# Three quarters of an MLP: weight halves made one chunk earlier on ScalarE, two VectorE steps reordered, one pair of loads moved

## The chip, the cores and the metric

The kernel runs on one core of one Trainium2 chip. The metric is the device time of one execution in microseconds (us). A core has five engines with instruction queues of their own: TensorE (PE, matrix products), VectorE (DVE), ScalarE (ACT), GpSimd (POOL) and SyncE (SP, which here issues nearly all DMA transfers). Each works through its own queue in order; they meet only at semaphores.

## The reference

Two transformer-like blocks run one after the other on 512 tokens of width 1024, in float32. The change touches only the MLP of the first block:

```python
u = rms_norm(h, norm_mlp_g[l])
h = h + jnp.square(jax.nn.relu(u @ w_mlp1[l])) @ w_mlp2[l]   # 1024 -> 4096 -> 1024
```

Around it stand a convolution branch, a latent attention and a cross attention before, and in the second block a spatial gating, a dilated attention and three projections after. All results must hold to float32 accuracy.

## The kernel before, in words

**Products in three parts.** TensorE multiplies in a rounded 32-bit format (F32R). To keep accuracy each operand is split in a high half (rounded, written by ACT with a Copy into `wh`, `fh`, `sh`, `s4h`) and a low half (the rest, written by DVE with a subtraction into `wl`, `fl`, `sl`, `s4l`). Each product is then three matmuls: high by high, low by high, high by low.

**Weights in chunks.** Weights stream in chunks of 512 KB (128 x 1024 floats). SP loads a chunk into `raw` (two slots), ACT's `split(c)` makes the high half in `wh[:, c % 4]`, DVE's `lower(c)` the low half in `wl[:, c % 4]`, PE uses them. The waits between: a load waits until the chunk that was in its slot has been lowered; `split` waits for the landing and until PE has entered the chunk behind the slot's last user (`chunk_entered`); `lower` waits for `split`; PE waits for `lower` (`lo_made`).

**The MLP in quarters.** The 4096 inner columns are done in four quarters q = 0 to 3, each an up part (`up{q}`) and a down part (`down{q}`).

An up part has eight jobs m = 0 to 7. PE's job is 24 matmuls into bank `lin0` or `lin1` in turn. Then ACT takes the bank with a Relu into `ta` or `tb` (`to(...)`, which also frees the bank), DVE squares it into `tc` or `td`, ACT copies the high half into `fh`, DVE subtracts for `fl`. After each odd job DVE makes sums of the pair of activation tiles (`sums`, into `first_turned`), ACT copies their high halves (`fh`, `sh`, `s4h`), and DVE makes their low halves one job later (`sums_low`).

The down parts of quarters 0 to 2 (`seven`) use a Strassen-like scheme with seven products in place of eight, for which DVE also makes sums of pairs of weight tiles (`pair_sums(u, kk)`, kk = 0 to 3, three additions each). Such a down part has 14 chunks, called v0 to v13 here, of 12 matmuls each; v0, v2, v4, v6 are a raw tile, v1, v3, v5, v7 are a sum and half of a tile, v8 to v13 the rest. The raw tiles come over a ring of four slots (`raw2`, `raw3`, `raw[:, 1]`, `raw[:, 0]`; the trace calls them all `raw`), loaded by `seven_loaded(u, r)`, r = 0 to 11. v(2k) and v(2k+1) can be made only after pair_sums(k). PE's v1 writes both `lin` banks, so it also waits until both are free, which the Relu of jobs 6 and 7 does. The fourth quarter is plain.

**What sets the order.** All orders are written out by hand in the program of each engine. In the up part of quarters 0 to 2, chunk c+m is the one that job m uses, and c+8 is v0 of the down part. Before the change ACT's job m is: split(c+m+3), Relu, copy of `fh`, and after odd jobs the three copies of the sums. DVE's job m is: lower(c+m+3), in some jobs pair_sums, then sums_low, the square, sums, the low half. So v0, v1 and v2 are made within the up part, and v3 and on behind it.

Of the kernel before, what the change touches and what calls it, by code (L numbers as in the profile page):

```python
# [30 lines left out]
ACT = mybir.ActivationFunctionType  # L31
AX_X = mybir.AxisListType.X

P = 128
# [48 lines left out]
NORM_NO = {n: k for k, (n, _) in enumerate(NORMS)}  # L83
# [8 lines left out]
ADD0, _t = {}, 0  # L92
# [30 lines left out]
SEVENS = 3  # L123
# [26 lines left out]
def seven_lowered(u, r):  # L150

    return SEVEN0[u] + r + (r > 9) + 1


def seven_sum(u, kk, n):

    return SEVEN_SUMS * u + (3 * kk + n if n < 4 else 12 + kk + 1)
# [34 lines left out]
def build(nc, a, out):  # L192
    ctx = ExitStack()
    with ctx:
# [3 lines left out]
        def sb(name, shape, dt=F32, stack=ctx):  # L198
            return stack.enter_context(nc.sbuf_tensor(name, shape, dt))
# [14 lines left out]
        st = ExitStack()  # L214
# [105 lines left out]
        crows = sb("crows", [TAPS, CONV], stack=st)  # L320
        st.close()
        st = ExitStack()
        s4h = sb("s4h", [P, 4, 256], F32R, st)
        s4l = sb("s4l", [P, 4, 256], F32R, st)
        acc5 = sb("acc5", [P, 2, S], stack=st)
        raw2 = sb("raw2", [P, 1024], stack=st)
        st.close()
        st = ExitStack()
        xq = sb("xq", [P, XH, S], F32R, st)
# [191 lines left out]
        def _(sp):  # L521
# [98 lines left out]
            for q in range(4):  # L620
                c, _ = phase(f"up{q}")
                for m in range(DT):
                    if q and m < 2:
                        sp.wait_ge(sums_made, seven_sum(q - 1, 2 + m, 4))
                    load(c + m, a["w_mlp1"][0], q * FFQ + P * m, DT, P)
                    if 0 < q < SEVENS and m == 5:
                        for r in range(2):
                            sp.wait_ge(lo_made, seven_lowered(q - 1, 8 + r))
                            sp.wait_ge(sums_made, seven_sum(q - 1, r, 4))
                            seven_loaded(q, r)  # L630
                c, _ = phase(f"down{q}")
                rows = a["w_mlp2"][0][q * FFQ:(q + 1) * FFQ, :]
                if q == SEVENS:
                    for m in range(DT):
                        load(c + m, rows, P * m, DT, P)
                    continue
                for r in range(2 if q else 0, SEVEN_LOADS):
                    if r < 2:
                        sp.wait_ge(std_made, NORM_NO["mlp"] + 1)
                    elif r < 4:  # L640
                        sp.wait_ge(lo_made, c.static + r - 3)
                    else:
                        sp.wait_ge(lo_made, seven_lowered(q, r - 4))
                        if r % 2 == 0:
                            sp.wait_ge(sums_made, seven_sum(q, (r - 4) // 2, 3))
                    seven_loaded(q, r)
# [716 lines left out]
        def _(act):  # L1363
# [55 lines left out]
            def to(j, dst, func, rows=slice(0, P), n=S, **kw):  # L1419

                act.activation(dst, read(j)[rows, 0:n], func, **kw).then_inc(lin_freed[j.slot(2)], 1)
# [266 lines left out]
            def up(q):  # L1688
                c, j = phase(f"up{q}")
                for m in range(DT):  # L1690
                    if q == SEVENS or m == 0:
                        split(c + (m + 2))
                    if q < SEVENS:
                        split(c + (m + 3))
                    to(j + m, (ta, tb)[m % 2][:], ACT.Relu)
                    n = 256 if q < SEVENS and m % 2 == 0 else S
                    act.wait_ge(f_sq, DT * q + m + 1)
                    act.activation(fh[:, m, 0:n], (tc, td)[m % 2][:, 0:n], ACT.Copy).then_inc(f_high, 1)
                    if q < SEVENS and m % 2:
                        kk = m // 2  # L1700
                        act.wait_ge(s_made, 4 * q + kk + 1)
                        act.activation(fh[:, m - 1, 256:512], SF[:, 0, :], ACT.Copy)
                        act.activation(sh[:, kk, :, :], SF[:, 1:3, :], ACT.Copy)
                        act.activation(s4h[:, kk, :], SF[:, 3, :], ACT.Copy).then_inc(s_high, 1)
                    if q == 0 and m == 3:
                        norm_std("mlp")

            for q in range(4):
                up(q)
                c, _ = phase(f"down{q}")  # L1710
                if q < SEVENS:
                    for v in range(3, 10):
                        split(c + v)
                    if q == 0:
                        part_copied(0, SUM_X1, PART_X)
                        part_copied(1, SUM_Q1, PART_Q)
                    split(c + 10)
                    if q == 0:
                        part_copied(2, SUM_P, PART_P)
                        part_copied(3, SUM_R1, PART_R)  # L1720
                    for v in range(11, 16):
                        split(c + v)
                    if q == 0:
                        part_copied(4, SUM_X2, PART_X)
                        part_copied(5, SUM_Q2, PART_Q)
                        part_copied(6, SUM_R2, PART_R)
                    continue
                for m in range(DT):
                    if m == 0:
                        split(c + 2)  # L1730
                    if m < DT - 1:
                        split(c + (m + 3))
                    act.wait_ge(h_added, DT + m + 1)
                    wait(act, hsq_added, 2 * m + 1)
                    src = h[:, m, :]
                    gain_high(uh[:, m, :], src, both[:, m:m + 1])
                    act.activation(ta[:], src, ACT.Square).then_inc(hsq_made, 1)
                    act.activation(tb[:], src, ACT.Square, scale=col("final_norm_g", m)).then_inc(hsq_made, 1)
# [182 lines left out]
        def _(dve):  # L1921
# [493 lines left out]
            def up(q):  # L2415
                c, j = phase(f"up{q}")
                for m in range(DT):
                    if q == SEVENS or m == 0:
                        lower(c + (m + 2))
                    if q == 0 and m == 5:  # L2420
                        pair_sums(q, 0)
                    if q < SEVENS:
                        lower(c + (m + 3))
                    if 0 < q < SEVENS and m == 3:
                        pair_sums(q, 0)
                    if q < SEVENS and m == (5 if q else 6):
                        pair_sums(q, 1)
                    base = SEVEN_PARTS * SEVENS
                    if q == SEVENS and m == 0:
                        dve.wait_ge(part_taken, base)  # L2430
# [22 lines left out]
                    r_, whole, n = (ta, tb)[m % 2][:], (tc, td)[m % 2], 256 if q < SEVENS and m % 2 == 0 else S  # L2453
                    dve.tensor_tensor(whole[:], r_, r_, ALU.mult).then_inc(f_sq, 1)
                    dve.wait_ge(f_sq, DT * q + m + 1)
                    if q < SEVENS and m % 2:
                        sums(q, m // 2)
                    low(fl[:, m, 0:n], whole[:, 0:n], fh[:, m, 0:n], f_high, DT * q + m + 1, f_low)
# [17 lines left out]
            def seven(u):  # L2476

                c, _ = phase(f"down{u}")
                lower(c + 3)
                sums_low(u, 3)  # L2480
                pair_sums(u, 2)
                lower(c + 4)
                lower(c + 5)
                pair_sums(u, 3)
                for v in range(6, 10):
# [352 lines left out]
```

## Time and profile before

| | us |
|---|---|
| median of 3 runs (1355.49 to 1355.65) | 1355.64 |
| the profiled execution | 1355.72 |
| its span, first to last instruction | 1354.0 |
| PE busy in the span | 1327.3 (98%) |
| DVE busy | 1039.1 (77%) |
| ACT busy | 626.8 (46%) |
| mean granted TensorE clock | 0.996 |

The profile tells for each engine when it was busy and, from semaphore events, which instruction ended its idle time. A matmul's recorded duration (0.39 us) is longer than the distance between two starts (0.23 us), since matmuls overlap; distances of starts are what counts for time. Busy shares over the whole span say little of a single place: one has to look at the stretch in which PE stands still and read what ended each wait.

### The profile page before, as it was taken

What the parts mean: (1) busy time and instruction counts of PE and PEld (TensorE: products, weight loads), DVE (VectorE), ACT (ScalarE), POOL (GpSimd) and SP (SyncE); (2) the same over time, 40 slices, a digit from 0 to 9 for tenths busy, and PEclk for the clock granted to TensorE, in tenths of its full rate; (3) what the DMA queues carried; (4) which work ended last, traced back from release to release, by engine and by line L of the source; (5) the groups of instructions that cost most, each with busy time, mean ns of one, the idle gap of its engine ahead of it and who ended that gap; (6) DMA issues with size and microseconds to landing.
All of it is one profiled execution on the core that took longest, in us unless ns stands there. A gap on an engine that the chain in (4) does not pass through costs nothing.

```text
span 1354.0 us, 17136 instructions
## 1 busy us (share of the span) xinstructions
PE 1327.3 (98%) x6357; PEld 1085.4 (80%) x6357; DVE 1039.1 (77%) x1715; ACT 626.8 (46%) x1076; POOL 62.7 (5%) x60
## 2 busy tenths in 40 slices
PE   7999999999999899999999999999999999999998
PEld 6787877788888778788788888878888888888886
DVE  7868888885677766877887564598889988995685
ACT  7535655564555454434434544734333434333234
POOL 1000000102002000000001500000000000000000
PEclk9999999999999999999999999999999999999999
DMA  5333332243323234342333333322233223223332
GB/s 163 94 93 78 77 74 84 64 139 109 94 94 107 88 117 125 96 138 70 101 109 94 94 109 93 93 84 82 82 98 90 86 68 96 85 76 109 96 108 93
DMA packets 204340, 130.33 MB, mean 96 GB/s; under 512 B 21426, under 2 KB 190467, under 8 KB 204258
## 3 DMA queue, kind: packets, MB, share of 16 engines
q1 hardware_dynamic: 202642, 126.62, 32.1%
q10 hardware_dynamic: 1616, 2.62, 0.6%
q8 instruction: 51, 0.84, 0.3%
q14 instruction: 31, 0.25, 0.1%
HBM read 127.12 MB, written 2.10 MB: 95 GB/s over the span
## 4 chain that ended last, share of the span: by engine, by line
PE 86%; DVE 8%; ACT 4%; issue 2%; ACTq 0%; DVEq 0%
PE lin L757 21%; PE lin L761 20%; PE lin L760 20%; PE ob L1254 1%; PE sc L849 1%; PE sc L1113 1%; PE sc L1117 1%; PE sc L1116 1%; DVE wl L1965 1%; PE sc L1210 1%; PE sc L1213 1%; PE sc L1214 1%; ACT wh L1390 1%; PE tr L862 1%; PE ob L886 1%
## 5 line engine op out<-in xcount | busy, mean ns | idle before, releaser
L1965 DVE TENSOR_TENSOR wl<-raw,wh 128x1024 fp32r<-128x1024 f32 (+2 forms) x211 | 251.8, 1195 | 70.4 <-ACT wh L1413 69.4
L1413 ACT ACTIVATE wh<-raw 128x1024 fp32r<-128x1024 f32 (+2 forms) x211 | 214.8, 1020 | 92.9 <-DMA raw<-in_w_mlp_dram 23.3
L757 PE MATMUL lin<-uh,wh 128*128 128x512 f32 x624 | 250.4, 401 | 1.0 <-DVE ul L2037 0.9
L761 PE MATMUL lin<-uh,wl 128*128 128x512 f32 x624 | 243.4, 390 | 0.0
L760 PE MATMUL lin<-ul,wh 128*128 128x512 f32 x624 | 243.1, 390 | 0.0
L757 PE MATMUL lin<-vh,wh 128*128 128x512 f32 x512 | 202.6, 396 | 0.2 <-DVE te L2700 0.2
L760 PE MATMUL lin<-vl,wh 128*128 128x512 f32 x512 | 199.6, 390 | 0.0
L761 PE MATMUL lin<-vh,wl 128*128 128x512 f32 x512 | 199.3, 389 | 0.0
L757 PEld LDWEIGHTS lin<-uh,wh 128*128 128x128 f32 x624 | 117.2, 188 | 28.2 <-issue 3.8
L760 PEld LDWEIGHTS lin<-ul,wh 128*128 128x128 f32 x624 | 117.3, 188 | 24.9 <-issue 2.2
L761 PEld LDWEIGHTS lin<-uh,wl 128*128 128x128 f32 x624 | 117.1, 188 | 24.9
L757 PEld LDWEIGHTS lin<-vh,wh 128*128 128x128 f32 x512 | 96.2, 188 | 24.5 <-issue 4.2
L761 PEld LDWEIGHTS lin<-vh,wl 128*128 128x128 f32 x512 | 96.1, 188 | 20.3
L760 PEld LDWEIGHTS lin<-vl,wh 128*128 128x128 f32 x512 | 96.2, 188 | 18.9
L2658 DVE STREAM_TRANSPOSE first_turned<-logit 32x320 f32<-32x320 f32 x128 | 64.3, 503 | 2.2
L2658 DVE STREAM_TRANSPOSE second_turned<-logit 32x320 f32<-32x320 f32 x128 | 64.3, 502 | 1.8
L1460 ACT ACTIVATE logit<-logit,small 128x128 f32<-128x128 f32 (+1 forms) x96 | 53.3, 558 | 19.7 <-DVE small L2046 19.4
L2144 DVE SCALAR_TENSOR_TENSOR conv<-conv,taps 128x512 f32<-128x512 f32 x60 | 44.9, 748 | 0.0
L2144 DVE SCALAR_TENSOR_TENSOR te<-conv,taps,te 128x512 f32<-128x512 f32 x56 | 41.8, 747 | 0.0
L1390 ACT ACTIVATE wh<-raw 128x1024 fp32r<-128x1024 f32 x24 | 25.4, 1058 | 31.6 <-DVE raw L1932 22.1
L1950 DVE TENSOR_TENSOR wl<-raw,wh 128x1024 fp32r<-128x1024 f32 x24 | 29.4, 1224 | 7.7 <-ACT wh L1390 7.6
L2046 DVE CUSTOM_DVE_ANT_0 logit<-sc,bias 128x128 f32<-128x128 f32 (+1 forms) x64 | 28.7, 488 | 4.5 <-PE sc L849 4.0
(666 smaller groups left out, 2499.0 us busy)
## 6 DMA issues: line engine op xcount, KB each, us to landing
raw<-in_w_in_dram SPq DMA_DIRECT2D x100, 512.0 KB, 3.8
raw<-in_w_mlp_dram SPq DMA_DIRECT2D x64, 512.0 KB, 4.0
raw<-in_w_out_dram SPq DMA_DIRECT2D x16, 512.0 KB, 3.5
raw<-in_w_xkv_dram SPq DMA_DIRECT2D x8, 512.0 KB, 3.6
raw<-in_w_proj_b_dram SPq DMA_DIRECT2D x8, 512.0 KB, 3.7
raw<-in_w_proj_a_dram SPq DMA_DIRECT2D x8, 512.0 KB, 3.6
raw<-in_w_mlp_dram SPq DMA_DIRECT2D x12, 256.0 KB, 2.6
xtok<-in_x_dram ACTq DMA_DIRECT2D x4, 512.0 KB, 4.9
```

The source lines that it names most:

```text
L757: ins = pe.matmul(o, wh[:, slot, at], xh_, start=start, stop=False)
L760: pe.matmul(o, wh[:, slot, at], xl_, start=False, stop=False)
L761: return pe.matmul(o, wl[:, slot, at], xh_, start=False, stop=stop)
L849: ins = pe.matmul(sc[b][:, o:o + KEYS[q]], qt[:, q * P:(q + 1) * P], keys[:, 0:KEYS[q]], start=True, stop=True)
L1390: act.activation(high, raw_, ACT.Copy).then_inc(hi_made, 1)
L1413: act.activation(wh[:, c.slot(4), 0:size], raw[:, c.slot(2), 0:size], ACT.Copy).then_inc(hi_made, 1)
L1460: act.activation(p, p, ACT.Exp, bias=nmax[:, q:q + 1], scale=-1.0, accum_out=den[:, q:q + 1])\
L1950: dve.tensor_tensor(low_, raw_, high, ALU.subtract).then_inc(lo_made, 1)
L1965: dve.tensor_tensor(wl[:, c.slot(4), 0:size], raw[:, c.slot(2), 0:size], wh[:, c.slot(4), 0:size].bitcast(F32), ALU.subtract).then_inc(lo_ ...
L2046: dve.tensor_tensor_reduce(logit[:, LOFF[q]:LOFF[q] + KEYS[q]], banks[q][:, o:o + KEYS[q]], bias[:, S - KEYS[q]:S], 1.0, 3e38, ALU.add, AL ...
L2144: return dve.scalar_tensor_tensor(at, zt, tap_, at, ALU.mult, ALU.add)
L2658: ins = dve.transpose(BLOCKS[p][32 * k:32 * k + 32, :, 32 * q:32 * q + 32], probs[32 * q:32 * q + 32, :, k, :])
```

## The change

In the up parts of quarters 0 to 2:

- ACT makes the high half of the next chunk right behind each Relu instead of ahead of it, and that of chunk c+m+4 instead of c+m+3. v3 is made at job 7, and v4 behind the last copy of `fh`; the copies of the last activation sums stand behind v4.
- DVE's order in jobs 0 to 6 keeps lower(c+m+3) first. pair_sums(0) is at job 3 and pair_sums(1) at job 5 in all three quarters (in quarter 0 they were at jobs 5 and 6), and both stand behind that job's lower. In job 7 lower of v3 and pair_sums(2) now stand between the square and the activation sums.
- SP issues the first pair of raw tiles of quarter 0 at job 5's load, as in the other quarters, once the sum of squares of the norm is complete, instead of behind all eight loads and after the standard deviation. For this the buffer `raw2` was moved to another place of the shared memory region.

PE's, POOL's and the fourth quarter's programs are as before, and every engine has the same instructions in number and kind.

```diff
@@ the shared memory region
+        raw2 = sb("raw2", [P, 1024], stack=st)
         s4h = sb("s4h", [P, 4, 256], F32R, st)
         s4l = sb("s4l", [P, 4, 256], F32R, st)
         acc5 = sb("acc5", [P, 2, S], stack=st)
-        raw2 = sb("raw2", [P, 1024], stack=st)
@@ SP
                     load(c + m, a["w_mlp1"][0], q * FFQ + P * m, DT, P)
-                    if 0 < q < SEVENS and m == 5:
+                    if q < SEVENS and m == 5:
                         for r in range(2):
-                            sp.wait_ge(lo_made, seven_lowered(q - 1, 8 + r))
-                            sp.wait_ge(sums_made, seven_sum(q - 1, r, 4))
+                            if q:
+                                sp.wait_ge(lo_made, seven_lowered(q - 1, 8 + r))
+                                sp.wait_ge(sums_made, seven_sum(q - 1, r, 4))
+                            elif r == 0:
+                                sp.wait_ge(sq_added, ADD0["mlp"] + NTILES["mlp"] - 1)
                             seven_loaded(q, r)
...
-                for r in range(2 if q else 0, SEVEN_LOADS):
-                    if r < 2:
-                        sp.wait_ge(std_made, NORM_NO["mlp"] + 1)
-                    elif r < 4:
+                for r in range(2, SEVEN_LOADS):
+                    if r < 4:
                         sp.wait_ge(lo_made, c.static + r - 3)
@@ ACT
                     if q == SEVENS or m == 0:
                         split(c + (m + 2))
+                    if q < SEVENS and m == 0:
+                        split(c + 3)
+                    to(j + m, (ta, tb)[m % 2][:], ACT.Relu)
                     if q < SEVENS:
-                        split(c + (m + 3))
-                    to(j + m, (ta, tb)[m % 2][:], ACT.Relu)
+                        split(c + (m + 4))
                     n = 256 if q < SEVENS and m % 2 == 0 else S
                     act.wait_ge(f_sq, DT * q + m + 1)
                     act.activation(fh[:, m, 0:n], (tc, td)[m % 2][:, 0:n], ACT.Copy).then_inc(f_high, 1)
+                    if q < SEVENS and m == 7:
+                        split(c + 12)
...
-                    for v in range(3, 10):
+                    for v in range(5, 10):
                         split(c + v)
@@ DVE
-                    if q == 0 and m == 5:
-                        pair_sums(q, 0)
                     if q < SEVENS:
                         lower(c + (m + 3))
-                    if 0 < q < SEVENS and m == 3:
-                        pair_sums(q, 0)
-                    if q < SEVENS and m == (5 if q else 6):
-                        pair_sums(q, 1)
+                    if q < SEVENS and m in (3, 5):
+                        pair_sums(q, m // 4)
...
                     dve.wait_ge(f_sq, DT * q + m + 1)
+                    if q < SEVENS and m == 7:
+                        lower(c + 11)
+                        pair_sums(q, 2)
                     if q < SEVENS and m % 2:
                         sums(q, m // 2)
...
                 c, _ = phase(f"down{u}")
-                lower(c + 3)
+                lower(c + 4)
                 sums_low(u, 3)
-                pair_sums(u, 2)
-                lower(c + 4)
                 lower(c + 5)
                 pair_sums(u, 3)
```

ACT's rows at the end of quarter 1's up part, before: from the Relu of job 6 (`ta<-lin0`) on. `wh<-raw` is v2, `logit` and `raw` are v3, `raw2` is v4.

```order
L1421 ACTIVATE ta<-lin0 128x512
L1698 ACTIVATE fh<-tc 128x256
L1390 ACTIVATE wh<-raw 128x1024
L1421 ACTIVATE tb<-lin1 128x512
L1698 ACTIVATE fh<-td 128x512
L1702 ACTIVATE fh<-first_turned 128x256
L1703 ACTIVATE sh<-first_turned 128x512
L1704 ACTIVATE s4h<-first_turned 128x256
L1382 ACTIVATE wh<-logit 128x512
L1383 ACTIVATE wh<-raw 128x512
L1390 ACTIVATE wh<-raw2 128x1024
```

The same place on ACT now.

```order
L1422 ACTIVATE ta<-lin0 128x512
L1391 ACTIVATE wh<-raw 128x1024
L1701 ACTIVATE fh<-tc 128x256
L1422 ACTIVATE tb<-lin1 128x512
L1383 ACTIVATE wh<-logit 128x512
L1384 ACTIVATE wh<-raw 128x512
L1701 ACTIVATE fh<-td 128x512
L1391 ACTIVATE wh<-raw2 128x1024
L1707 ACTIVATE fh<-first_turned 128x256
L1708 ACTIVATE sh<-first_turned 128x512
L1709 ACTIVATE s4h<-first_turned 128x256
```

v2 stands behind the Relu of job 6 and no longer between that Relu's `fh` copy and the Relu of job 7; v3 and v4 stand ahead of the copies of the last sums.

DVE's rows at the same place, before: from the square of job 7 (`td<-tb`) to the low half of v4 (`wl<-raw2`). `first_turned` are the activation sums, `trig<-raw2,raw3` is the last addition of pair_sums(2).

```order
L2454 TENSOR_TENSOR td<-tb 128x512
L2402 TENSOR_TENSOR first_turned<-tc,td 128x256
L2403 TENSOR_TENSOR first_turned<-first_turned,tc 128x256
...
L1978 TENSOR_TENSOR fl<-td,fh 128x512
L1946 TENSOR_TENSOR wl<-logit,wh 128x512
L1947 TENSOR_TENSOR wl<-raw,wh 128x512
...
L2397 TENSOR_TENSOR s4l<-first_turned,s4h 128x256
L1930 TENSOR_TENSOR raw3<-raw2,raw3 128x512
L1932 TENSOR_TENSOR raw2<-raw2 128x512
L1934 TENSOR_TENSOR trig<-raw2,raw3 128x512
L1950 TENSOR_TENSOR wl<-raw2,wh 128x1024
```

The same place on DVE now.

```order
L2455 TENSOR_TENSOR td<-tb 128x512
L1951 TENSOR_TENSOR wl<-logit,wh 128x512
L1952 TENSOR_TENSOR wl<-raw,wh 128x512
L1935 TENSOR_TENSOR raw3<-raw2,raw3 128x512
L1937 TENSOR_TENSOR raw2<-raw2 128x512
L1939 TENSOR_TENSOR trig<-raw2,raw3 128x512
L2407 TENSOR_TENSOR first_turned<-tc,td 128x256
...
L1983 TENSOR_TENSOR fl<-td,fh 128x512
L1955 TENSOR_TENSOR wl<-raw2,wh 128x1024
L2400 TENSOR_TENSOR fl<-first_turned,fh 128x256
```

The low half of v3 and pair_sums(2) stand ahead of the activation sums, and the low half of v4 right behind the low half of the last activation tile.

## Rows read from the trace of the kernel before

**Rows 1.** The page: engines busy, and the chain that ended last.

```profile
PE 1327.3 (98%) x6357; PEld 1085.4 (80%) x6357; DVE 1039.1 (77%) x1715; ACT 626.8 (46%) x1076; POOL 62.7 (5%) x60
...
PE 86%; DVE 8%; ACT 4%; issue 2%; ACTq 0%; DVEq 0%
```

**Rows 2.** Stretches: the three seven-product down parts; length, then each engine's busy time, PEclk.

```profile
463.40:509.07 45.67, 40.22 (x170) 32.43 (x168) 32.40 (x47) 23.78 (x38) 0.00 (x0) 0.96 0.34 105
552.59:596.39 43.80, 40.75 (x170) 32.48 (x168) 35.75 (x53) 17.68 (x25) 0.00 (x0) 0.96 0.35 108
639.91:682.05 42.14, 39.07 (x170) 31.30 (x168) 35.19 (x53) 17.54 (x25) 0.99 (x2) 1.00 0.34 109
```

**Rows 3.** Timeline of PE: start, duration, instruction, idle time before it and its releaser.

```profile
469.90 0.76 PE L1113 MATMUL lin<-wh,sh 128*128 128x512 f32 x1 [3.62 <-ACT tb L1421]
481.60 0.47 PE L1113 MATMUL sc<-wh,fh 128*128 128x512 f32 x1 [1.83 <-DVE wl L1950]
...
562.20 0.50 PE L1113 MATMUL lin<-wh,sh 128*128 128x512 f32 x1 [0.95 <-DVE wl L1947]
567.24 0.47 PE L1113 MATMUL sc<-wh,fh 128*128 128x512 f32 x1 [2.03 <-DVE wl L1950]
...
569.28 0.63 PE L1116 MATMUL sc<-wh,fl 128*128 128x512 f32 x1
...
585.41 0.39 PE L1113 MATMUL tr<-wh,fh 128*128 128x512 f32 x1
...
596.39 0.39 PE L757 MATMUL lin<-uh,wh 128*128 128x512 f32 x1
```

**Rows 4.** Timeline of ACT, jobs 6 and 7 of quarter 1.

```profile
550.21 0.58 ACT L1421 ACTIVATE ta<-lin 128x512 f32<-128x512 f32 x1
553.55 0.42 ACT L1698 ACTIVATE fh<-tc 128x256 fp32r<-128x256 f32 x1 [2.76 <-DVE tc L2454]
553.87 1.05 ACT L1390 ACTIVATE wh<-raw 128x1024 fp32r<-128x1024 f32 x1
554.82 0.58 ACT L1421 ACTIVATE tb<-lin 128x512 f32<-128x512 f32 x1
```

**Rows 5.** Timeline of DVE, jobs 6 and 7 of quarter 1 and its down part.

```profile
550.34 0.69 DVE L1946 TENSOR_TENSOR wl<-vtok,wh 128x512 fp32r<-128x512 f32 x1 [1.76 <-ACT wh L1383]
...
556.81 0.42 DVE L2402 TENSOR_TENSOR first_turned<-tc,td 128x256 f32<-128x256 f32 x1
...
560.85 0.69 DVE L1946 TENSOR_TENSOR wl<-logit,wh 128x512 fp32r<-128x512 f32 x1 [1.76 <-ACT wh L1383]
...
565.87 1.23 DVE L1950 TENSOR_TENSOR wl<-raw,wh 128x1024 fp32r<-128x1024 f32 x1 [0.40 <-ACT wh L1390]
```

**Rows 6.** One line of the kernel, L536 (chunk loads), then L617 (raw tiles).

```profile
DMA to landing us min/median/max: 3.3/3.8/5.5
...
DMA to landing us min/median/max: 2.5/3.3/5.3
```

**Rows 7.** Timeline of ACT, POOL and DVE near the start of quarter 0.

```profile
425.04 0.60 ACT L1421 ACTIVATE ta<-lin 128x512 f32<-128x512 f32 x1 [1.27 <-PE lin L761]
...
428.38 1.06 ACT L1413 ACTIVATE wh<-raw 128x1024 fp32r<-128x1024 f32 x1 [1.56 <-DMA raw<-in_w_mlp_dram]
430.48 0.60 ACT L1421 ACTIVATE tb<-lin 128x512 f32<-128x512 f32 x1 [1.04 <-PE lin L761]
...
421.65 1.42 POOL L708 TENSOR_TENSOR logit<-logit,qt 128x512 f32<-128x512 f32 x1 [1.14 <-ACT qt L1432]
...
422.56 2.73 DVE L1965 TENSOR_TENSOR wl<-raw,wh 128x1024 fp32r<-128x1024 f32 x2 [0.66 <-ACT wh L1413]
...
446.82 3.35 DVE L2014 RECIPROCAL logit<-logit 128x512 f32<-128x512 f32 x1 [1.29 <-ACT logit L1439]
```

**Rows 8.** Timeline of SP: the first pair of raw tiles, quarter 1 then quarter 0.

```profile
514.62 1.00 SPq L617 DMA_DIRECT2D raw<-in_w_mlp_dram  x2
...
446.81 1.29 SPq L617 DMA_DIRECT2D raw<-in_w_mlp_dram  x3
```

## The prediction

> **What bounds the kernel now.** I read the page first. PE is busy 98% of the span and stands for 86% of the chain that ended last, DVE for 8% and ACT for 4% [rows 1]. So only what makes PE wait, or slows its clock, costs time. The waits of PE sorted by time then led me to the down parts of quarters 0 to 2, and the stretches put a size on them: they contain the same 168 matmuls each but last 45.67, 43.80 and 42.14 us [rows 2]. The reader is to see three different lengths for the same work.
>
> What would it be without a wait? The end of quarter 1's down part is undisturbed: from the first matmul of v10 (585.41) to the first of the next up part (596.39) are four chunks of 12, 48 matmuls in 10.98 us, 0.2288 us each [rows 3]. 168 of them are 38.4 us. The excess is 7.3, 5.4 and 3.7 us, together 16.4 us.
>
> The timeline of PE says where it sits. Quarter 0: 3.62 us before v1, until ACT's Relu frees `lin1`, and 1.83 us before v4. Quarter 1: 0.95 us before v3 and 2.03 us before v4, both until DVE has the low half [rows 3]; quarter 2 waits as quarter 1 does, with PE busy 39.07 of 42.14 us. The rest of the excess is the clock: it is 0.96 over the first two stretches and 1.00 over the third [rows 2]; 4% of 45.67 and 43.80 is 1.8 us each. After the wait at 567.24 matmuls take 0.63 us instead of 0.39 for a while [rows 3], the 1.2 GHz level instead of 2.4. So 11.6 us of idle time (lengths less PE busy in rows 2), 3.6 us of clock, and 1.2 us in matmuls that start slowly behind a wait: 16.4 us again.
>
> Why is DVE late? It is a round trip. Behind each odd job ACT copies the sums, only then makes the next weight half, and DVE sits idle 1.76 us for it (550.34, 560.85) [rows 5]. Meanwhile ACT itself waits for DVE: 2.76 us before the `fh` copy of job 6, and the weight half v2 then stands ahead of the Relu of job 7, which starts at 554.82 although PE was done at 552.59 [rows 4, 2]. PE jobs end every 5.44 us, as Relus that wait only for PE show (425.04, 430.48) [rows 7].
>
> **The change part by part.** No instruction is added or removed, so the sum consists of waits only. I walk quarter 1 with durations from rows. A DVE operation takes 1.23 us at 1024 wide, 0.69 at 512, 0.42 at 256, ACT 1.05 at 1024 and 0.6 at 512; where the next one has nothing to wait for it starts about 0.1 us before that is over (553.87 to 554.82) [rows 4, 5].
>
> *Next half right behind the Relu.* The half that DVE needs first in job m+1 is there before DVE has finished job m. The 1.76 us wait goes in each odd job. DVE's work in two jobs is then, at those rates, lowers 2.3, sums_low 1.3, squares 1.4, sums 1.6, low halves 1.1 and a wait of 0.6 for `fh`: 8.3 us of 10.88, and 10.3 with pair sums; so it keeps up with PE. Followed from 514: DVE begins the square of job 4 at about 537.1, of job 6 at 548.0, and the Relu of job 7 starts at PE's end plus 0.2, 552.8, instead of 554.82. The low half of v2 is done at about 550.8.
>
> *v3, pair_sums(2), v4.* From that Relu's end (553.4) DVE does: square 0.7 (554.1), a wait for v3's halves from ACT (554.5), v3 1.3 (555.7), pair_sums(2) 2.05 (557.8), activation sums 1.6 (559.4), low half of the last tile 0.6 (560.0), v4 1.1 (561.1). ACT makes v4 at 557.2, behind the second pair addition. The copies of the last sums wait for DVE until 559.4 and end at 560.7. DVE goes on with sums_low 1.3 (562.4), v5 1.2 (563.6), two pair additions (565.0), ACT's v6 1.06 (566.1), v6 1.23 (567.3), v7 (568.6).
>
> PE without waits enters v1 at 555.3, v2 558.1, v3 560.85, v4 563.6, v5 566.4, v6 569.2. It needs v3 from 555.7, v4 from 561.1, v5 from 563.6, v6 from 567.3: slack 5.1, 2.5, 2.8 and 1.9 us. The third sums are needed at v6, 569.2, and are ready at 562.4. So what was late by 0.95 and 2.03 is early, and the thinnest cover is 1.9 us at v6. Behind v7 ACT is paced by `chunk_entered`, hence by PE, and all moves up with it. Term: 5.4 us for quarter 1, 3.7 for quarter 2, whose stream is the same.
>
> *Quarter 0.* The same with three more things. DVE has to split the total of squares (1.1 us) and take the 3.35 us reciprocal, which waits for ACT until 446.82 [rows 7]. The chain to it (Relu of job 3, square, sums, copies, deviation) keeps its place within 0.2 us, so job 4's square is at 452.4, as before. But pair_sums(0), 2 us, is already done then, and both 1.76 us waits behind it are gone. I get job 6's square at 462.5, the Relu of job 7 at 463.6 instead of 469.18, v3 ready 467.0 (needed 471.7), v4 472.4 (474.5), v5 474.8 (477.3), v6 478.5 (480.0). Slack 1.5 us at v6. v1 is entered at 466.2. Term: 7.3 us, but with the thinnest cover.
>
> *The moved pair of loads.* In quarter 0 raw tiles 0 and 1 (512 and 256 KB) were issued at 446.81 and now follow job 5's load, which goes out when DVE has lowered c+3, at 422.56 + 2.73 = 425.3 [rows 8, 7]. Their new wait, the sum of squares, is over when POOL ends its last addition, 421.65 + 1.42 = 423.07 [rows 7]: nothing is held. Behind them on SP stands the load of c+6, which must wait for lower(c+4) at about 431.4 anyway, so the two issues, 1.00 us [rows 8], hide.
>
> *ACT is now held where it was free.* The first half behind a Relu (c+4) waits for its DMA until 428.38 [rows 7]; now the `fh` copy of job 0 is queued behind it, 3 us later than before, and DVE's lower(c+4) about 0.7 us later. Relu 1 is due only at 430.48. Cost nothing here. In general a chunk must land before the Relu that precedes it: from lower(c+m+2) to landing the median is 3.8 us and the worst 5.5 [rows 6]. A round over two jobs is Relu 0.6, square and sums 2.3, low half 0.6, lower 1.2, landing 3.8 to 5.5: 8.5 to 10.2 us of 10.88. It closes with 0.7 us at the worst landing.
>
> The rows for quarter 1 show the same burst (a chunk and the pair, issued together at 514.62) without a wait of PE in that up part [rows 8, 3]. In quarter 0 it comes while c+4 and c+5 are in flight; if that makes c+4 land at 5.5 instead of 3.8 us [rows 6], DVE, which has no pause from c+4 to the reciprocal, is 1.7 us late and the slack of 1.5 at v6 is gone: a rival, below.
>
> The Trainium skill (DMA: Bandwidth & Descriptors, section "Two DMAs through the same engine are not ordered") says that nothing orders transfers across the engines that carry them, so a later transfer may hold up an earlier one. By that rule the burst can delay c+4 though it was issued behind it; by first in, first out it could not. No run here shows which.
>
> **Sum.** 1355.72 (the profiled execution, 1.7 around a span of 1354.0) less 7.3, 5.4 and 3.7 gives 1339.3. The profiled run is 0.08 above the median of 1355.64, which is nothing. The unknown is the cover: if each quarter keeps a wait as large as its slack estimate may be wrong (2 us, a third of the DVE waits removed), 6 us come back: 1345.3. The other end: nothing but these stalls can go, so 1338.
>
> **Rivals.**
> *A part of the stall stays, at v4 or v6.* pair_sums(2), 2.05 us, stands ahead of the activation sums, and v6 hangs on pair_sums(3), which is as late as ever in DVE's queue. For it: quarter 0's slack of 1.5 us and semaphore hops that I took at 0.03. Against: slack of 1.9 in quarters 1 and 2. Price: 1 us in each quarter plus a dropped clock of 1.8 in one is 4.8 us: 1344. Chance 15%.
> *The pair holds up c+4 in quarter 0.* For it: three transfers of 512 KB and one of 256 share the engines, and landings range from 3.3 to 5.5. Against: quarter 1 has that burst and no wait. Price: 1.7 late less 1.5 of slack, 0.2 us, and up to 0.5 with a slow start behind the wait: 1339.7. Chance 10%.
> *The round trip only moves.* The Relu is on time, but the `fh` copy is now behind a 1 us half, so low halves and sums slide and DVE waits there what it saved. Then only the 3.62 before v1 and its clock go, and half of the others: 5.4 + 2.5 = 8: 1348. Against it: ACT has the time, at 46% busy. Chance 6%.
> *Slower: a chunk's landing holds ACT.* ACT is in order, and a half waiting for its DMA now sits between a Relu and its `fh` copy, jobs 0 to 3. It decides once landing takes over 6.2 us (10.88 less 4.7). At 8 us, each two jobs lose 1.8 and the bank is freed late; twice per quarter, with a clock drop of 1.8 and the old stalls of 16.4 coming back behind it, is 3 x 5.4 = 16 us over and all of the gain: 1355 to 1358. Against: the worst landing is 5.5 [rows 6]. Chance 3%.
> *It does not do what it says* (a wait elsewhere orders the halves as before): 1355.6, chance 2%.
>
> **How the numbers follow.** The forecast, no stall or at most 1 us in all, 1338.3 to 1341, has 64%, and the pair in quarter 0, whose time lies in the same stretch, 10%. 0.2% is 2.7 us, about what a measurement of this kernel can tell from no change. Faster: 74 + 15 + 6 = 95%, less 1 for overlap, 94%; same 3%; slower 3%. The range goes from 1338.0 to 1345.5, with the first rival inside; outside remain about 11%.
>
> **What would show it.** Right: the three down parts last 38.3 to 38.8 us each, PE waits for nothing over 0.3 us between jobs 6 and v7, the clock is 1.00 in all three, the Relu of job 7 starts within 0.3 us of PE's end, and DVE's 1.76 us waits are gone. Wrong: a PE wait for `wl` before v4 or v6; a wait of DVE for the halves behind a DMA in jobs 0 to 3; a Relu that comes behind a half. If the down parts are short and the total is not, the time was given back in quarter 3 or behind it.

## The result and the profile after

The changed kernel takes 1338.91 us (median of 4 runs, 1338.52 to 1338.94), the kernel before 1355.64 us (1355.49 to 1356.11, 4 runs): ratio 0.9875, 95% interval 0.9858 to 0.9892, faster by 16.7 us. Its profiled execution took 1338.94 us. The forecast was 1339.3.

The page of the changed kernel, the lines that answer to [rows 1]: engines busy, and the chain that ended last.

```profile
PE 1321.7 (99%) x6357; PEld 1083.4 (81%) x6357; DVE 1037.5 (78%) x1715; ACT 625.1 (47%) x1076; POOL 62.8 (5%) x60
...
PE 96%; DVE 2%; ACT 1%; issue 0%; ACTq 0%; DVEq 0%
```

PE's share of the chain rose from 86 to 96%, DVE's fell from 8 to 2. DVE and ACT are as busy as they were: nothing was taken off them, they are only no longer what PE waits for.

The same three down parts as in [rows 2] (length, busy time of PE, PEld, DVE, ACT, POOL, then PEclk, DMA share, GB/s):

```profile
463.45:501.72 38.27, 38.27 (x169) 31.53 (x168) 27.76 (x39) 22.75 (x37) 0.00 (x0) 1.00 0.39 119
545.24:583.51 38.27, 38.27 (x170) 31.53 (x168) 33.09 (x49) 16.18 (x23) 0.00 (x0) 1.00 0.36 112
627.03:665.29 38.26, 38.26 (x169) 31.53 (x168) 33.04 (x49) 16.18 (x23) 0.99 (x2) 1.00 0.36 112
```

Three equal lengths, each filled by PE to the last hundredth, at a granted clock of 1.00. Together 114.80 us where there were 131.61 [rows 2]: 16.8 us, which is all that the time moved by (16.73). The up parts between them last 43.52 us in both kernels, and quarter 3 and what is behind it kept its length too. PE waits for nothing from 400 us to the end of the third down part. At the four places of [rows 3] that had a wait stand plain matmuls. Here v1, v4 and v6 of quarter 0, then v3, v4 and v6 of quarter 1, first matmul of each (timeline of PE):

```profile
466.18 0.39 PE L1114 MATMUL lin<-wh,sh 128*128 128x512 f32 x1
...
474.33 0.39 PE L1114 MATMUL sc<-wh,fh 128*128 128x512 f32 x1
...
479.77 0.39 PE L1114 MATMUL sc<-wh,fh 128*128 128x512 f32 x1
...
553.40 0.39 PE L1114 MATMUL lin<-wh,sh 128*128 128x512 f32 x1
...
556.12 0.39 PE L1114 MATMUL sc<-wh,fh 128*128 128x512 f32 x1
...
561.56 0.39 PE L1114 MATMUL sc<-wh,fh 128*128 128x512 f32 x1
```

ACT in jobs 6 and 7 of quarter 1, to be laid beside [rows 4]:

```profile
540.50 1.05 ACT L1391 ACTIVATE wh<-raw 128x1024 fp32r<-128x1024 f32 x1
541.44 0.41 ACT L1701 ACTIVATE fh<-tc 128x256 fp32r<-128x256 f32 x1
545.44 0.60 ACT L1422 ACTIVATE tb<-lin 128x512 f32<-128x512 f32 x1 [3.59 <-PE lin L762]
```

Before, the Relu of job 7 came 2.2 us after PE's end, behind a wait for DVE and a half of the weights. Now ACT sits idle 3.59 us until PE is done and starts 0.20 us later (PE's down part begins at 545.24). DVE, same place and the down part behind it, beside [rows 5]:

```profile
546.07 0.69 DVE L2455 TENSOR_TENSOR td<-tb 128x512 f32<-128x512 f32 x1 [2.56 <-ACT tb L1422]
547.18 0.69 DVE L1951 TENSOR_TENSOR wl<-logit,wh 128x512 fp32r<-128x512 f32 x1 [0.42 <-ACT wh L1384]
...
552.63 1.22 DVE L1955 TENSOR_TENSOR wl<-raw,wh 128x1024 fp32r<-128x1024 f32 x1
...
555.64 0.68 DVE L1952 TENSOR_TENSOR wl<-raw,wh 128x512 fp32r<-128x512 f32 x1
...
558.78 1.23 DVE L1955 TENSOR_TENSOR wl<-raw,wh 128x1024 fp32r<-128x1024 f32 x1 [0.40 <-ACT wh L1391]
```

The 1.76 us waits for a weight half are gone; what DVE waits for now, 2.56 us, is PE's next product by way of the Relu: slack. The rows give v3 ready at 548.5, v4 at 553.85, v5 at 556.3, v6 at 560.0. Against the PE rows above, v6 has 1.55 us of slack in quarter 1 and, lowered at 477.70 + 1.23 = 478.93 there, 0.84 us in quarter 0.

The start of quarter 0, beside [rows 7, 8]: ACT, DVE, then the queue of SP.

```profile
428.30 1.06 ACT L1414 ACTIVATE wh<-raw 128x1024 fp32r<-128x1024 f32 x1 [2.61 <-DMA raw<-in_w_mlp_dram]
...
430.54 0.60 ACT L1422 ACTIVATE tb<-lin 128x512 f32<-128x512 f32 x1 [0.86 <-PE lin L762]
```

```profile
429.77 0.43 DVE L1983 TENSOR_TENSOR fl<-tc,fh 128x256 fp32r<-128x256 f32 x1 [3.35 <-ACT fh L1701]
...
446.69 3.35 DVE L2019 RECIPROCAL logit<-logit 128x512 f32<-128x512 f32 x1 [1.29 <-ACT logit L1440]
```

```profile
425.77 1.56 SPq L617 DMA_DIRECT2D raw<-in_w_mlp_dram x2
```

The chunk c+4 lands in time for ACT at 428.30, before it was 428.38: the two raw tiles issued at 425.77 did not hold it up. Their own landing took 6.4 us where 5.3 was the longest of such before [rows 6], and nobody waited for it (L617 between 420 and 430 us):

```profile
DMA to landing us min/median/max: 6.4/6.4/6.4
```

The chunk behind c+4, c+5, was issued at 425.36, 0.4 us ahead of the pair. It landed later than before (L536 from 425.3 to 425.6 us, the kernel before and the changed one):

```profile
DMA to landing us min/median/max: 5.1/5.1/5.1
...
DMA to landing us min/median/max: 5.6/5.6/5.6
```

In the seven traces with the pair behind it, those of the experiments below included, c+5 took 5.05 to 5.58 us, in the four without it 4.69 to 5.07; no wait of PE came of it.

DVE does wait 3.35 us for the `fh` copy of job 0 that is now queued behind the half of c+4; the reciprocal starts at 446.69, before at 446.82.

### The profile page after: what moved, and what is told of

Same layout as the page of the kernel before. It is cut to its first block, busy times and chain, and to the rows that moved or that the text cites. A ratio compares the mean times of both kernels' runs of the same rounds, so it can differ in the third digit from the quotient of the medians.

```text
span 1337.2 us, 17139 instructions
## 1 busy us (share of the span) xinstructions
PE 1321.7 (99%) x6357; PEld 1083.4 (81%) x6357; DVE 1037.5 (78%) x1715; ACT 625.1 (47%) x1076; POOL 62.8 (5%) x60
## 4 chain that ended last, share of the span: by engine, by line
PE 96%; DVE 2%; ACT 1%; issue 0%; ACTq 0%; DVEq 0%
PE lin L758 23%; PE lin L762 23%; PE lin L761 23%; PE ob L1255 1%; PE sc L850 1%; PE sc L1118 1%; PE sc L1117 1%; PE sc L1114 1%; PE sc L1211 1%; PE sc L1214 1%; PE tr L1114 1%; PE tr L1117 1%; PE tr L1118 1%; PE sc L1215 1%; PE tr L863 1%; PE ob L887 1%
```

## The experiments

Two theories stood against each other. Mine: the cause is the round trip between ACT and DVE inside the up quarter, which needs the half to be four chunks ahead. The rival: the new tail of job 7 (v3, the third pair's sums and v4 drawn ahead) carries the gain. Further kernels ask whether the Relu's place alone does it, whether the quarters are independent, what the early pair is worth, and how much slack is left. All times are medians of 4 runs unless another number stands there. The median of before went from 1354.4 to 1355.7 us between groups of runs (what the traces show of it: last section), so I read the parts in the traces before the totals.

**The tail undone.**

```diff
-                    if q < SEVENS and m == 7:
-                        split(c + 12)
-                    if q < SEVENS and m == 7:
-                        lower(c + 11)
-                        pair_sums(q, 2)
...
+                lower(c + 3)
                 sums_low(u, 3)
+                pair_sums(u, 2)
+                lower(c + 4)
```

(ACT's split of v4 goes behind the sum copies.)

> The changed kernel with its tail of job 7 put back: v3's lower half and the third pair's sums stand behind the activation sums again, and ScalarE's split of v4 behind the sum copies; Relu first and four chunks ahead stay, and so does the early first pair. My theory (the round trip between ScalarE and VectorE is the cause, and the tail only leaves slack): VectorE is free for v3 at about 463.9+0.6+1.4+0.6 us in the first quarter, v3 comes some 1.5 us later than now against a slack of 4 us and more, v4 about as now, v6 0.3 us later at most, so 1338.9 to 1339.6 us, no wait of TensorE above 0.3 us. Rival (the tail carries a part of the gain): v4 or v6 is late in each of the three down parts by 1 us or more, and the time is 1342 to 1345 us.

1339.37 us, ratio 0.9888 (0.9871 to 0.9904). The down parts:

```profile
462.98:501.78 38.80, 38.55 (x170) 31.46 (x168) 27.84 (x39) 22.91 (x37) 0.00 (x0) 1.00 0.38 118
545.30:583.56 38.26, 38.26 (x169) 31.54 (x168) 33.00 (x49) 16.18 (x23) 0.00 (x0) 1.00 0.35 109
627.08:665.35 38.27, 38.27 (x169) 31.53 (x168) 33.10 (x49) 16.18 (x23) 0.99 (x2) 1.00 0.35 110
```

A wait of 0.25 us before v4 in quarter 0 and nothing in the others: without the tail all but 0.5 us of the gain is there. My theory holds, the rival falls. Whether the tail is worth even the 0.5 isn't shown: in this trace the part begins 0.47 us earlier than in the changed kernel (462.98, there 463.45) and ends only 0.06 later (501.78, there 501.72).

**The tail alone**, in the kernel before:

```diff
                     to(j + m, (ta, tb)[m % 2][:], ACT.Relu)
+                    if q < SEVENS and m == 7:
+                        split(c + 11)
...
+                    if q < SEVENS and m == 7:
+                        split(c + 12)
...
+                    if q < SEVENS and m == 7:
+                        lower(c + 11)
+                        pair_sums(q, 2)
```

(and the same calls taken from their old places.)

> The kernel before with the new tail of job 7 alone (ScalarE splits v3 right behind relu 7 and v4 right behind the last high half, VectorE lowers v3 and makes the third pair's sums ahead of the activation sums); the order of the other jobs, three chunks ahead and the place of the first pair stay as before. My theory: job 7 itself stays late by the round trips of the jobs before it (relu 7 of the first quarter at 469.18 us, five microseconds behind its product), so the first quarter keeps the larger part of its stall, and the other two keep 0.5 to 1 us each with part of the clock loss: 1344 to 1348 us. Rival (the tail carries the gain): 1338.9 to 1341 us. Second rival (the tail is worth nothing): 1355 us.

1347.54 us, ratio 0.9949 (0.9932 to 0.9965), inside my 1344 to 1348. Down parts of 43.70, 39.65 and 39.65 us; the second and third keep 1.4 us each where I had expected 0.5 to 1. The waits of PE in its trace:

```profile
PE lin L1113 <- ACT tb L1421: 3.6, 1, 3.6
PE sc L1113 <- DVE wl L1954: 0.7, 2, 0.4
PE sc L1113 <- DVE acc L2476: 0.2, 1, 0.2
```

The 3.6 us before v1 stay, to the tenth; the waits at v3 and v4 go, and one of 0.35 us at v6 appears. So the tail by itself gives 8.6 us of the parts (131.61 less 123.00), and the rest of the change by itself 16.3 (131.61 less 115.33). Both figures contain the fall of the clock in quarter 1 of before, 1.7 us, which not every execution of before seems to have (last section); by the medians of this group of runs they are 6.9 and 15.0. The two are not added: each removes the same waits at v3 and v4, and whichever comes second finds them gone.

**Relu first, but three chunks ahead:**

```diff
-                    if q < SEVENS and m == 0:
-                        split(c + 3)
                     to(j + m, (ta, tb)[m % 2][:], ACT.Relu)
                     if q < SEVENS:
-                        split(c + (m + 4))
+                        split(c + (m + 3))
```

(with the tail of before).

> The changed kernel with Relu ahead of the next high half in every job, but three chunks ahead instead of four, and the tail of job 7 as before. My theory: it is the distance and not the order alone that breaks the round trip; now the split of chunk m+3 waits behind relu m for the product that it is two jobs ahead of, VectorE gets it later, and each job of the up quarters has a smaller lead: slower than the changed kernel by 5 to 30 us, that is 1344 to 1369 us, with waits of TensorE inside the up quarters, which neither kernel has. Rival (Relu first is all that matters): 1338.9 to 1342 us.

1372.78 us, ratio 1.0136 (1.0119 to 1.0153), 4 us beyond my upper end: the direction was right, the size too small. The place was wrong as well: I had expected waits inside the up quarters, and there is only one, of 1.22 us in quarter 0; the up parts of quarters 1 and 2 still last 43.52 us, and the loss is in the down parts. Quarter 1's down part, then ACT ahead of it and at its start:

```profile
556.79:605.51 48.72, 42.33 (x169) 33.61 (x168) 37.78 (x57) 19.84 (x30) 0.00 (x0) 0.93 0.30 96
...
549.02 0.58 ACT L1422 ACTIVATE tb<-lin 128x512 f32<-128x512 f32 x1
549.50 1.05 ACT L1391 ACTIVATE wh<-raw 128x1024 fp32r<-128x1024 f32 x1
554.50 0.63 ACT L1699 ACTIVATE fh<-td 128x512 fp32r<-128x512 f32 x1 [3.94 <-DVE td L2451]
...
562.54 0.58 ACT L1422 ACTIVATE tb<-lin 128x512 f32<-128x512 f32 x1
```

DVE needs that half (549.50) before it may do the square of the same job, and here also a set of pair sums stands between; ACT waits 3.94 us for the square. The Relu of job 7 then comes (562.54) 5.8 us after PE (556.79), and each down part opens with 3.6 us of wait (5.1 in quarter 0). The clock falls behind these waits too: 0.93 in each of the three parts. In quarters 1 and 2, where the place of the Relu is all that differs from before, a down part lasts 48.72 us against 43.80 and 42.14. The place of the Relu alone is worth less than nothing: at this distance it delays what DVE needs next.

**Four ahead, but the half before the Relu:**

```diff
+                    if q < SEVENS:
+                        split(c + (m + 4))
                     to(j + m, (ta, tb)[m % 2][:], ACT.Relu)
-                    if q < SEVENS:
-                        split(c + (m + 4))
```

> The changed kernel, four chunks ahead and with the new tail, but with the split of chunk m+4 ahead of relu m in each job of the first three up quarters, as the split stood ahead of the Relu before. Each split waits for the product of job m, so relu m starts some 1.1 us (1.07 us of splitting) after its product instead of 0.2 us. My theory (the distance is what breaks the round trip, the order only gives about 1 us of slack): the chain behind relu 7 is 1.1 us later, against slacks of 1.0 us at v6 of the first quarter and some 1.5 us elsewhere: 1338.9 to 1341 us, at most one or two waits of 0.3 us and less in a down part. Rival (Relu first is what removes the stall at the sums): waits of 2 us and more in each down part, 1345 us or more.

1339.85 us, ratio 0.9885 (0.9869 to 0.9902), down parts of 39.08, 38.36 and 38.35 us. One wait is left in the three quarters:

```profile
466.57 0.47 PE L1114 MATMUL lin<-wh,sh 128*128 128x512 f32 x1 [0.50 <-DVE wl L1955]
```

The profile names DVE, but the matmul writes `lin`, and the Relu that frees it ran from 465.85 to 466.42. The Relu was 1.9 to 2.2 us later than in the changed kernel, not 1.1: the split waits for its slot as well. In quarter 1 it starts 1.0 us after PE's end, the Relu 0.2. So distance is what breaks the round trip, and the Relu's place is worth some 0.9 us on top (1.0 by the parts). Four ahead with the half first and the tail of before was not run, so how far the tail covers here is not shown. The wait is 0.2 us longer than I allowed for and at v1, not at v6: I had thought of the chain behind the Relu and not of the bank.

**The new order in the first quarter alone** (`if q == 0` on each of the new lines, `q > 0` on the old ones).

> The changed kernel with the new order of ScalarE and the new tail in the first quarter alone; the second and third quarters have the order of before. My theory: the three quarters are independent, the first gives its 7.3 us back and the others keep their 5.4 and 3.7 us: 1348.3 us, down parts of 38.3, 43.8 and 42.1 us. Rival (what one quarter loses is carried into the next, so that mending the first mends part of the others): below 1345 us. Second rival (the clock's fall in the second and third hangs on the stall in the first): the waits stay, the clock of the second and third down parts is 1.00, 1345 to 1346 us.

1347.48 us, ratio 0.9949 (0.9933 to 0.9966). Stretches:

```profile
463.43:501.70 38.27, 38.27 (x170) 31.53 (x168) 27.74 (x39) 22.78 (x37) 0.00 (x0) 1.00 0.38 119
545.22:587.30 42.08, 39.13 (x169) 31.31 (x168) 35.07 (x53) 17.54 (x25) 0.00 (x0) 1.00 0.34 110
630.82:672.91 42.09, 39.06 (x169) 31.31 (x168) 35.05 (x53) 17.53 (x25) 0.99 (x2) 1.00 0.35 109
```

The first quarter gives its whole excess, the other two keep the waits of 0.92 to 0.95 and 1.99 to 2.03 us at v3 and v4: the quarters don't carry anything over. The second is 42.08, not 43.80: no fall of the clock in this execution. **The same kernel traced again** asks whether that was chance:

> The kernel with the new order in the first quarter alone once more, for its trace. Its four times were 1346.59, 1346.73, 1348.22 and 1348.26 us, and the first, of which there is a trace, had no fall of the clock. If one fall of the clock is the difference of 1.6 us, this execution lies at 1346.6 us without one or at 1348.2 us with one in the second or third down part, then 43.7 us long in place of 42.1 us, with the waits unchanged.

1346.66 us (one run), clock 1.00, parts of 38.27, 42.14 and 42.12 us, no fall, as the 1346.6 us case expects. The two executions at 1348.2 have no trace; their mean clock over the span was 0.997 where it was 1.000 in the two at 1346.6. So in both traces the waits of quarters 1 and 2 stand at a clock of 1.00, as the second rival has it (its time of 1345 to 1346 us is 0.6 short), and only the clock of the two untraced executions speaks against it: whether the stall in the first quarter makes a later fall more likely stays open. And **the kernel before again**:

> The kernel before once more, for its trace. In the first trace the granted clock fell behind the 2.03 us wait of the second down part (43.80 us) and not behind the same wait of the third (42.14 us). If the fall comes by chance from execution to execution, the waits are the same here, and the three down parts are 45.67, 43.80 and 42.14 us with 1.7 us more or less where a fall comes or stays away; if it hangs on what the kernel did before, the three lengths are the same as then.

1356.72 us (one run):

```profile
462.90:510.15 47.25, 40.68 (x169) 32.44 (x168) 32.58 (x47) 23.78 (x38) 0.00 (x0) 0.96 0.33 102
553.67:595.82 42.15, 39.11 (x169) 31.30 (x168) 35.15 (x53) 17.54 (x25) 0.00 (x0) 1.00 0.35 109
639.34:683.05 43.71, 40.69 (x169) 32.47 (x168) 35.67 (x53) 17.65 (x25) 0.99 (x2) 0.96 0.34 108
```

Now the third part has the fall and the second has none [rows 2], with the same waits in both. Behind a 2 us wait it comes in one execution and stays away in the next. Quarter 0 has its fall at another place, right behind the wait at v4 (ended 481.06) and not behind the one at v1, and it waits 0.95 at v3 and 2.03 at v4 where there was 1.83 at v4 alone: its length is 47.25, not the 45.67 of the first trace, with one fall in both.

**The early pair undone**, in quarter 0 alone:

```diff
-                    if q < SEVENS and m == 5:
+                    if 0 < q < SEVENS and m == 5:
                         for r in range(2):
...
-                for r in range(2, SEVEN_LOADS):
-                    if r < 4:
+                for r in range(2 if q else 0, SEVEN_LOADS):
+                    if r < 2:
+                        sp.wait_ge(std_made, NORM_NO["mlp"] + 1)
...
-                    if q < SEVENS and m in (3, 5):
-                        pair_sums(q, m // 4)
+                    if q < SEVENS and m in (3 if q else 4, 5):
+                        pair_sums(q, m // 5)
```

> The changed kernel with the first quarter's first pair of raw tiles loaded where it was before, behind the reciprocal's result, and its sums at job 4 in place of job 3; nothing else undone. My theory: the first pair's place frees VectorE for the reciprocal's chain, the jobs behind it come 1 to 1.7 us later against a slack of 1.0 us at v6 of the first quarter (lowered 478.93, entered 479.9 us): 0 to 1 us over the changed kernel, 1338.9 to 1339.9 us, the first down part alone longer than 38.27 us. Rival (the early pair matters): a stall of 2 us and more and a clock below 1.00 in the first down part, 1341 to 1344 us.

1340.00 us, ratio 0.9887 (0.9871 to 0.9904), a tenth above my upper end; the first down part lasts 39.37 us, the others 38.26 and 38.27. DVE stood 1.7 us later from job 4 on (its square at 454.15, in the changed kernel 452.49), and PE waited 0.47 us at v6. The early pair, with its sums at job 3 instead of 4, is worth 1.1 us.

**How much slack is left.** Extra additions of 128x512 on DVE, ahead of v5's lower half in each of the three down parts, two of them and then four:

```diff
+                dve.wait_ge(hi_made, (c + 6).v())
+                for k in range(2):
+                    step(dve.tensor_tensor(wl[:, (c + 5).slot(4), 0:512], h[:, k, :], h[:, k, :], ALU.add))
                 lower(c + 5)
```

> The changed kernel with two subtractions' worth of extra work on VectorE in each of the first three down parts (two additions of 128x512, one behind the other, about 0.72 us each, ahead of v5's lower half). It measures the slack that is left at v6: 1.0 us in the first quarter, 1.7 in the second and third. My theory: 1.44 us of work, a wait of 0.4 to 0.5 us in the first down part and none in the others: 1339.3 to 1339.5 us. Rival (there is much more slack than the ends of the rows say, or less): no change at all, or 1.44 us in each, 1343.2 us.

> The same with four such additions, 2.9 us in each down part. My theory: 1.9 us of waits in the first down part and 1.2 us in each of the others, 4.3 us in all, 1343.2 us, and up to 2 us more if the granted clock falls behind one of these waits, as it did behind the 2.03 us wait of the second down part before: 1343.2 to 1345.2 us. Rival (PE's wait at v6 is made up for later in the part): below 1341 us.

Two: 1341.14 us, parts of 39.21, 38.86 and 38.86. Four: 1345.34 us, parts of 40.66, 40.31 and 40.33. Their excess over 38.27 is 2.1 and 6.5 us where I had expected 0.45 and 4.3, and both times lie above what I had written, without any fall of the clock. The waits of PE with four:

```profile
PE sc L1114 <- DVE wl L1955: 2.3, 3, 0.8
PE lin L1114 <- DVE wl L1952: 1.6, 3, 1.1
PE sc L1114 <- DVE acc L2473: 0.2, 1, 0.2
```

Idle time is 4.1 us, near my 4.3, though v5 now shares it with v6. The other 2.4 us are what a wait costs beside its idle time. The rows of quarter 0, v5:

```profile
478.27 0.50 PE L1114 MATMUL lin<-wh,sh 128*128 128x512 f32 x1 [1.06 <-DVE wl L1952]
478.61 0.39 PE L1117 MATMUL lin<-wh,sl 128*128 128x512 f32 x1
```

Starts come every 0.228 us in a row of matmuls; this one came 1.44 us after the one ahead of it, with 1.06 idle, and the next 0.34 later: 1.44 + 0.34 less 2 x 0.228 is 1.32, that is 0.26 us more than the idle time. Eight such waits are 2.1 of the 2.4 (the eighth, 0.15 us at `acc` in quarter 2, is too short for the view above). With two additions quarters 1 and 2 lose 0.59 us each, of which 0.18 is idle time in front of a bank that `part` evacuates (`acc`): 1.44 us of work less 0.18 of idle time, a slack of about 1.3 us that I had not looked at.

## Why the prediction was right

By its own steps:

- *38.4 us for an undisturbed down part, excess 7.3, 5.4 and 3.7.* Measured 38.27, 38.27, 38.26: the excess that went is 7.40, 5.53 and 3.88. The whole of the main term is right; 0.2288 us for a matmul was 0.2278.
- *11.6 of idle, 3.6 of clock, 1.2 of slow starts.* The idle time and the slow starts repeat in the second trace of before. Between the other two terms the sum was divided wrongly, which cancels: two falls of the clock at 1.66 us are 3.3, and the matmul starts show eight waits, two of them of 0.07 us at v1 that the views leave out, at some 0.25 us each, 2.0. And that there were two falls was the luck of one execution: in the second trace of before the fall had moved from quarter 1 to 2, and in another group of runs four executions of before were some 1.5 us faster.
- *The round trip is the cause and the 1.76 us waits go.* They went, and the tail undone, the tail alone, the distance of three and the half before the Relu show it from both sides.
- *Relu of job 7 at PE's end plus 0.2.* 0.20 in quarter 1 (545.44), 463.70 against 463.6 in quarter 0.
- *Quarter 1's slack: v3 5.1, v4 2.5, v5 2.8, v6 1.9 us.* 4.9, 2.3, 2.5 and 1.55: DVE's chain was 0.1 us longer than my additions, and PE came to its chunks up to 0.3 us sooner (v6 at 16.32 us into the part, where I had 16.6).
- *Quarter 0: job 6's square 462.5, v3 467.0, v4 472.4, v6 478.5, slack 1.5.* 462.66, 467.38, 472.77, 478.93, slack 0.84: right in order, but the thinnest cover was little more than half of what I gave it. The two additions found the same: a wait of 0.64 us in quarter 0, none at v6 in the others.
- *The moved pair costs nothing, and gives DVE room before the reciprocal.* With its sums a job earlier it gives 1.1 us.
- *The reciprocal keeps its place within 0.2 us.* It moved by 0.13.
- *A part of the stall stays at v4 or v6 (15%), or the round trip only moves (6%).* Neither: PE waits at no chunk. But at v6 of quarter 0 it was near, with 0.84 us.
- *The pair holds up c+4 (10%).* It did not: 428.30. The Trainium skill (DMA: Bandwidth & Descriptors, "Two DMAs through the same engine are not ordered") says that nothing orders transfers across the engines that carry them. Its section is about the order in which bytes are read and written; that a later transfer may hold up an earlier one was my inference. Here c+4, 1.5 us ahead of the pair, was untouched; c+5, 0.4 us ahead, took 5.6 us instead of 5.1, and ACT took it up at 431.03, 0.1 us after it landed. The sum made without such a delay was right.
- *A landing holds ACT (3%).* It would have decided from a landing of 6.2 us. Raw tiles took 6.4 and, in quarter 1, 6.5, but they stand before no Relu in these jobs; the slowest chunk took 5.6, and no wait of PE came of any.

Of the prediction's marks of being right all came: parts of 38.3 us, clock 1.00, no wait of PE, no time given back later. One of its marks of being wrong came too and meant nothing: in job 0 of each quarter DVE waits behind a half that waits for its DMA, longest 3.35 us in quarter 0, and has the slack for it.

What the forecast did not tell is how the gain is divided. It walked through the change as a whole; that the tail and the new distance remove the same waits, and that the tail is worth 0.5 us at most beside the rest, only the experiments show.

## What to carry to other kernels

When two engines feed a third and each waits for the other once a round, count how many rounds ahead the shared item is made: one more chunk of distance was worth 33 us here with the Relu first (1372.78 to 1339.37), and putting the Relu first was worth 0.9 us at four chunks and cost 18 at three (1354.4 to 1372.78, with the pair and sums of quarter 0 moved as well). Take the length of an undisturbed stretch from the trace and subtract: it gave the gain of this change to 0.5 us, before any thought on the cause. In these traces a wait costs its idle time and a quarter microsecond, so two short waits are dearer than one of their sum.

## What was not expected of the hardware

Whether the granted clock falls behind a given wait differs between executions of one kernel. The two traces of before have a wait of 1.83 to 2.03 us at v4 in each of their six down parts. Behind three of them matmuls go to the 1.2 GHz level (0.63 us each), the first of them starting 0.3 to 1.9 us after the wait, and for some 3 us; behind the other three they don't. Of four waits of 1.99 to 2.03 us with only the first quarter mended none was followed by a fall; of the three of 2.02 to 2.03 us at a distance of three, two were; of the five waits of 3.58 to 3.62 us that all these traces hold, four were; of those up to 1.2 us, none. One fall costs 1.66 us (43.80 less 42.14). That is also the step between executions of one kernel: in the first group of runs four of before took 1353.95 to 1354.40 us at a mean clock of 0.998 and three 1355.40 to 1355.52 at 0.996. The traces show falls in single down parts; that the steps in times without a trace are such falls is inferred from their size and clock. The changed kernel has no such waits left, and its four times lie within 0.42 us.

A fall also seems to hide part of the next wait: in quarter 0 of before, with the slow stretch behind the 3.62 us wait, only 1.83 us was left at v4; in the trace without one there the waits were 0.95 and 2.03 us.

Why the up part of quarter 0 begins 0.2 to 0.5 us earlier in some of the traces (418.98 us with the tail undone, 419.45 in the changed kernel) stays open. ACT's Relu of job 7 comes earlier with it (463.29, there 463.70), so it isn't shown that the earlier start is what PE then waits for at v4.
